# A 128x128 triangular inverse by doubling: 32x32 blocks in four row tiles for the first levels, and the even steps written out

## What is computed

```
def step(state, inp):
    rt, wt, kt, vt, kkt, at = inp
    sa = einsum('bhvk,bhk->bhv', state, -kkt)
    state = state * wt[:, :, None, :] + sa[..., None] * (kkt * at)[:, :, None, :] + vt[..., None] * kt[:, :, None, :]
    return state, einsum('bhvk,bhk->bhv', state, rt)
```

## Time and profile before

| | |
|---|---|
| median of three runs | 2680.56 us (2678.67 to 2683.04) |
| the profiled execution | 2677.95 us, span 2676.2 us |
| TensorE busy in the span | 2593.6 us, 97% |
| VectorE, ScalarE, GpSimd busy | 1908.0 (71%), 1268.7 (47%), 373.4 (14%) |
| chain that ended last | TensorE 88%, VectorE 7%, issue 2%, ScalarE 2% |
| even steps in the timeline | from 59.94 us (step 0) to 590.37 us |

### The profile page before, as it was taken

One profiled execution on the slowest core, in us unless ns is written; L12 is line 12 of the kernel. 1 busy time (PEld: TensorE's weight loads), 2 busy tenths in 40 slices (PEclk: granted clock), 3 DMA queues, 4 the chain that ended last, 5 costly groups with the idle time before them and its releaser, 6 DMA issues.

```text
span 2676.2 us, 48399 instructions
## 1 busy us (share of the span) xinstructions
PE 2593.6 (97%) x17454; PEld 2297.0 (86%) x17454; DVE 1908.0 (71%) x2983; ACT 1268.7 (47%) x1721; POOL 373.4 (14%) x376
## 2 busy tenths in 40 slices
PE   8998989989999999999999999998999999999998
PEld 8887888878888888888888888887888888888886
DVE  6666666666766666656789999997676666666666
ACT  6444444445554344334465555554555434433444
POOL 0111111112110011001112121111111001100112
PEclk9999999999999999999999999998999999999999
DMA  6222222234555555555454444443455555555543
GB/s 263 97 99 95 97 97 97 87 121 165 197 188 189 188 188 188 188 188 188 164 197 173 157 157 157 157 157 142 169 192 188 191 186 188 188 188 188 188 168 131
DMA packets 65866, 437.98 MB, mean 164 GB/s; under 512 B 9440, under 2 KB 10848, under 8 KB 17120
## 3 DMA queue, kind: packets, MB, share of 16 engines
q1 hardware_dynamic: 61920, 435.84, 46.1%
q10 hardware_dynamic: 3840, 0.70, 0.1%
HBM read 434.41 MB, written 2.10 MB: 163 GB/s over the span
## 4 chain that ended last, share of the span: by engine, by line
PE 88%; DVE 7%; issue 2%; ACT 2%; DMA 0%; DVEq 0%; ACTq 0%; SPq 0%; POOL 0%; POOLq 0%
PE acc L318 49%; PE acc L353 27%; PE acc L315 5%; PE mixer_banks L1593 2%; DVE w_low L308 1%; PE mixer_banks L1305 1%; PE mixer_banks L1397 1%; PE mixer_banks L1410 1%; ACT w_high L303 1%; ACT arena L651 0%; PE mixer_banks L1412 0%; PE acc L330 0%; DVE arena L1005 0%; DVE arena L993 0%; DVE arena L932 0%
## 5 line engine op out<-in xcount | busy, mean ns | idle before, releaser
L308 DVE TENSOR_TENSOR w_low<-w_raw,w_high 128x1024 fp32r<-128x1024 f32 x838 | 1053.1, 1258 | 413.3 <-ACT w_high L303 401.4
L303 ACT ACTIVATE w_high<-w_raw 128x1024 fp32r<-128x1024 f32 x837 | 881.6, 1058 | 938.8 <-PE acc L353 923.3
L318 PE MATMUL acc<-h_split,w_high 128*128 128x512 f32 x3840 | 977.0, 394 | 6.3 <-DVE arena L375 6.3
L318 PEld LDWEIGHTS acc<-h_split,w_high 128*128 128x128 f32 x3840 | 688.6, 189 | 128.4 <-issue 5.4
L353 PEld LDWEIGHTS acc<-h_split,w_low 128*128 128x128 f32 x4576 | 629.9, 191 | 39.7
L353 PE MATMUL acc<-h_split,w_low 128*128 128x256 f32 x4576 | 660.0, 282 | 0.0
L318 PE MATMUL acc<-mix_split,w_high 128*128 128x512 f32 x1908 | 493.0, 396 | 1.9 <-DVE mix_split L1267 1.4
L318 PEld LDWEIGHTS acc<-mix_split,w_high 128*128 128x128 f32 x1908 | 343.0, 190 | 64.7 <-issue 2.5
L480 POOL TENSOR_TENSOR arena<-arena,norm_scale 128x256 f32<-128x256 f32 x152 | 150.9, 993 | 1457.2 <-DVE arena L375 1456.0
L353 PEld LDWEIGHTS acc<-mix_split,w_low 128*128 128x128 f32 x1876 | 260.8, 191 | 21.3
L353 PE MATMUL acc<-mix_split,w_low 128*128 128x256 f32 x1876 | 267.1, 282 | 0.0
(11 more groups left out here) (257 smaller groups left out, 1684.1 us busy)
## 6 DMA issues: line engine op xcount, KB each, us to landing
w_raw<-w_gu SPq DMA_DIRECT2D x176, 1024.0 KB, 4.8
w_raw<-w_down SPq DMA_DIRECT2D x64, 1024.0 KB, 4.9
w_raw<-w_odd SPq DMA_DIRECT2D x64, 1024.0 KB, 4.8
w_raw<-w_even SPq DMA_DIRECT2D x49, 1024.0 KB, 4.8
w_raw<-w_down SPq DMA_DIRECT2D x32, 768.0 KB, 4.3
w_raw<-w_odd_out SPq DMA_DIRECT2D x16, 1024.0 KB, 4.8
w_raw<-w_even_out SPq DMA_DIRECT2D x10, 1024.0 KB, 4.8
w_raw<-w_even_out SPq DMA_DIRECT2D x6, 896.0 KB, 4.6
```

Of the source, the lines that this page charges most:

```text
L303: act.activation(wh[:, self.res, ks], raw[:, self.raw, ks], ACT.Copy).then_inc(high_done, 1)
L308: dve.tensor_tensor(wl[:, self.res, ks], raw[:, self.raw, ks], wh[:, self.res, ks].bitcast(F32), ALU.subtract).then_inc(low_done, 1)
L318: pe.matmul(acc[self.acc][:, 0:2 * T], wh[:, self.res, k], flat(both), start=k == 0, stop=stop)
```

## The change

- The inverse holds four diagonal 32x32 quarter blocks. Levels 1 to 4 are matmuls on four diagonal 32x32 tiles; `z` has 16 matmuls a level for 8, `txt` 32 for 16. `Xb`, `Zs`, `Ld` and the two halves of `TT` have half the columns. `Ld` is made by four copies for two. `m3` computes four quarter blocks for two half blocks.
- Level 5 becomes an off-diagonal block step like level 6: 8 matmuls in `z`, 12 in `txt`, three `tensor_scalar` pieces on VectorE. GpSimd spreads `TT` into `T11` (new, 64 rows) and `Tf` after level 4, two instructions for one; GpSimd's masking for level 5 is gone.
- `z` writes to bank 1 instead of bank 2, and the wait for `KTR` moves from `z(1)` to behind `z(6)`.
- ScalarE: the square of the keys (L612) comes before the table load and `high(3)`.
- VectorE: `evacuate(-1)` comes before `low(2)` instead of before `low(3)`.
- TensorE: `dense(16)` and `dense(16)` instead of `dense(8)` and `dense(24)`; in step 7 the second half of a block waits for `rw_end`.
- ScalarE and VectorE have all eight steps written out; GpSimd keeps its loop.

```
-        TT = take(4, 2, 64)
-        Xb = take(2, 4, 64)
-        Zs = take(4, 64)
-        Ld = take(4, 64)
+        TT = take(4, 2, 32)
+        Xb = take(2, 4, 32)
+        Zs = take(4, 32)
+        Zh = take(4, 64)
+        T11 = take(4, 64)
+        Ld = take(4, 32)
...
+        QUARTERS = [slice(q, q + 32) for q in range(0, P, 32)]
...
-                pool.wait_ge(S["rw_L"], 2 * j + 2)
-                for l in range(1, LEVELS - 1):
+                pool.wait_ge(S["rw_L"], 4 * j + 4)
+                for l in range(1, LEVELS - 2):
...
-                pool.wait_ge(S["rw_TT"], 7 * j + 6)
-                pool.tensor_tensor(Tf.rearrange("p n (a b) -> p n a b", a=2), TT[:, :, 1].unsqueeze(2).broadcast_to([P, 4, 2, 64]),
...
+                pool.wait_ge(S["rw_TT"], 9 * j + 5)
+                for out, rows, which, parts in ((T11, HALVES[0], 0, 2), (Tf, slice(0, P), 1, 4)):
+                    pool.tensor_tensor(out[rows].rearrange("p n (a b) -> p n a b", a=parts),
...
-                act.preload_act_table_set("natural_log_exp_and_others")
-
-                high(3)
                 act.wait_ge(S["rw_xv"], j + 1)
                 act.activation(d3[:, 2], xm[:, 1], ACT.Square, scale=pj[:, P_KK:P_KK + 1]).then_inc(S["rw_sq"], 1)
+                act.preload_act_table_set("natural_log_exp_and_others")
+                high(3)
...
-                for r in HALVES:
+                for r in QUARTERS:
                     act.activation(Ld[r], LTR[r, :, r], ACT.Copy).then_inc(S["rw_L"], 1)
...
+                    if l < LEVELS - 1:
+                        act.activation(flat(Zs), bank(1)[:, 0:P], ACT.Copy).then_inc(S["rw_Zs"], 1)
+                    else:
+                        act.activation(flat(Zh)[HALVES[1]], bank(1)[HALVES[1], 0:256], ACT.Copy).then_inc(S["rw_Zs"], 1)
...
-            even_step(0, even_block(0))
-            with act.Fori(0, 3) as i:
-                for e in range(2):
-                    even_step(1 + 2 * i + e, even_block(1 + e, i))
-            even_step(7, even_block(7), more=False)
+            for j in range(NRW):
+                even_step(j, even_block(j), more=j < NRW - 1)
...
+                evacuate(-1)
                 low(2)
...
-                evacuate(-1)
                 low(3)
...
+                    dve.wait_ge(S["rw_Tf"], 2 * j + 2)
+                    if l == LEVELS - 2:
+                        for out, rows, at in ((T11[:, :, 0:32], 1, 0), (Tf[:, :, 32:64], 0, P), (Tf[:, :, 96:P], 2, P)):
+                            rows = QUARTERS[rows]
+                            dve.tensor_scalar(out[rows], bank(0)[rows, at:at + P].rearrange("p (n c) -> p n c", n=4), -1.0, None, ALU.mult).then_inc(S["rw_TT"], 1)
...
+                            if ks[0] >= HALF:
+                                pe.wait_ge(S["rw_end"], NRW)
...
-                dense(8)
+                dense(16)
...
-                dense(24)
+                dense(16)
...
-                for b in range(2):
+                for b in range(4):
...
-                            last = pe.matmul(bank(4 + h)[HALVES[b], 64 * c:64 * c + 64], AR[rows, c, 0, HALVES[b]], bk[rows, 0, at], start=True, stop=True)
+                            last = pe.matmul(bank(4 + h)[QUARTERS[b], 32 * c:32 * c + 32], AR[rows, c, 0, QUARTERS[b]], bk[rows, 0, at], start=True, stop=True)
...
+                    if l == LEVELS - 2:
+                        for n in range(4):
+                            for q in (0, 2):
+                                r = QUARTERS[q]
+                                last = pe.matmul(bank(1)[QUARTERS[q + 1], 32 * n:32 * n + 32], LTR[r, n, QUARTERS[q + 1]], TT[r, n, 0], start=True, stop=True)
...
-                        for r in HALVES:
-                            last = pe.matmul(bank(2)[r, 64 * n:64 * n + 64], Xb[r, l % 2, n], TT[r, n, 0], start=True, stop=True)
+                        for r in QUARTERS:
+                            last = pe.matmul(bank(1)[r, 32 * n:32 * n + 32], Xb[r, l % 2, n], TT[r, n, 0], start=True, stop=True)
...
+                    if l == LEVELS - 2:
+                        low, high = QUARTERS[1], QUARTERS[3]
+                        for n in range(4):
+                            at = slice(P + 32 * n, P + 32 * n + 32)
+                            pe.matmul(bank(0)[low, 32 * n:32 * n + 32], TT[low, n, 1], Zs[low, n], start=True, stop=True)
+                            pe.matmul(bank(0)[QUARTERS[2], at], Zs[high, n], TT[high, n, 1], start=True, stop=True)
+                            last = pe.matmul(bank(0)[QUARTERS[0], at], Zs[low, n], TT[low, n, 1], start=True, stop=True)
...
-                        o = bank(0)[:, n * P:(n + 1) * P]
-                        for r in HALVES:
-                            pe.matmul(o[r, 0:64], TT[r, n, 1], Zs[r, n], start=True, stop=True)
-                        for r in HALVES:
-                            last = pe.matmul(o[r, 64:P], Zs[r, n], TT[r, n, 1], start=True, stop=True)
+                        o = bank(0)[:, n * 64:(n + 1) * 64]
+                        for r in QUARTERS:
+                            pe.matmul(o[r, 0:32], TT[r, n, 1], Zs[r, n], start=True, stop=True)
+                        for r in QUARTERS:
+                            last = pe.matmul(o[r, 32:64], Zs[r, n], TT[r, n, 1], start=True, stop=True)
...
+                waits(pe, 2 * j + 2, "rw_KTR")
                 pe.wait_ge(S["rw_kbn"], j + 1)
```

More of the change, by code:

```diff
@@ L39 @@
 C_HALF = C_CAUSAL + 3 * P
-C_LOW0 = C_HALF + 6 * 64
-C_IDH = C_LOW0 + 64
-C_END = C_IDH + 64
+C_LOW0 = C_HALF + 5 * 32
+C_IDQ = C_LOW0 + 32
+C_QUART = C_IDQ + 32
+C_END = C_QUART + P
 P_MU, P_W0, P_A0, P_KK, P_KA, P_RK = 0, 3, 4, 5, 6, 7
@@ L69, in shape_constants @@
         c[:, C_LVL + l * P:C_LVL + (l + 1) * P] = m
-        halves = lambda a: np.concatenate([a[:64, :64], a[64:, 64:]])
-        if l < 6:
-            c[:, C_HALF + 64 * l:C_HALF + 64 * (l + 1)] = halves(m)
+        quarters = lambda a: np.concatenate([a[q:q + 32, q:q + 32] for q in range(0, P, 32)])
+        if l < 5:
+            c[:, C_HALF + 32 * l:C_HALF + 32 * (l + 1)] = quarters(m)
         if l == 0:
-            c[:, C_LOW0:C_LOW0 + 64] = halves(m.T)
-            c[:, C_IDH:C_IDH + 64] = halves(np.eye(P))
+            c[:, C_LOW0:C_LOW0 + 32] = quarters(m.T)
+            c[:, C_IDQ:C_IDQ + 32] = quarters(np.eye(P))
+    c[:, C_QUART:C_QUART + P] = s // 32 == t // 32
     c[:, C_TRI:C_TRI + P] = s < t
@@ L995, in even_step @@
                 for h in range(2):
-                    dve.tensor_tensor(TT[:, 2 * h:2 * h + 2, 0], bank(4 + h)[:, 0:P].rearrange("p (c k) -> p c k", c=2),
-                                      bc(cst[:, C_LOW0:C_LOW0 + 64], 2), ALU.mult).then_inc(S["rw_T0"], 1)
-                dve.wait_ge(S["rw_L"], 2 * j + 2)
+                    dve.tensor_tensor(TT[:, 2 * h:2 * h + 2, 0], bank(4 + h)[:, 0:64].rearrange("p (c k) -> p c k", c=2),
+                                      bc(cst[:, C_LOW0:C_LOW0 + 32], 2), ALU.mult).then_inc(S["rw_T0"], 1)
+                dve.wait_ge(S["rw_L"], 4 * j + 4)
                 dve.tensor_tensor(TT[:, :, 1], Ld, bc(half_mask(0), 4), ALU.mult).then_inc(S["rw_T0"], 1)
@@ L1097, in _ @@
                 Block(EVEN + u + 2).low(dve, 1)
-            even_step(0, even_block(0))
-            with dve.Fori(0, 3) as i:
-                for e in range(2):
-                    even_step(1 + 2 * i + e, even_block(1 + e, i))
-            even_step(7, even_block(7), more=False)
+            for j in range(NRW):
+                even_step(j, even_block(j), more=j < NRW - 1)
             added = [KT]
@@ L1384, in z @@
                 def z(l):
-                    pe.wait_ge(S["rw_TT"], 7 * j + l)
+                    pe.wait_ge(S["rw_TT"], 9 * j + l)
                     if l == LEVELS - 1:
                         for n in range(4):
-                            last = pe.matmul(bank(2)[64:P, 64 * n:64 * n + 64], LTR[0:64, n, 64:P], TT[0:64, n, 0], start=True, stop=True)
+                            last = pe.matmul(bank(1)[64:P, 64 * n:64 * n + 64], LTR[0:64, n, 64:P], T11[0:64, n], start=True, stop=True)
                         last.then_inc(S["rw_Z"], 1)
                         return
-                    pe.wait_ge(S["rw_X"], 5 * j + l)
-                    if l == 1:
-                        pe.wait_ge(S["rw_KTR"], 2 * j + 2)
+                    if l == LEVELS - 2:
[3 more added lines that the diff above has]
+                                last = pe.matmul(bank(1)[QUARTERS[q + 1], 32 * n:32 * n + 32], LTR[r, n, QUARTERS[q + 1]], TT[r, n, 0], start=True, stop=True)
+                        last.then_inc(S["rw_Z"], 1)
+                        return
+                    pe.wait_ge(S["rw_X"], 4 * j + l)
                     for n in range(4):
-                        for r in HALVES:
-                            last = pe.matmul(bank(2)[r, 64 * n:64 * n + 64], Xb[r, l % 2, n], TT[r, n, 0], start=True, stop=True)
+                        for r in QUARTERS:
```

(8 more changed lines are left out.)

25 lines of the change are left out of this document (12 added, 13 removed).

## The result

The changed kernel takes 2659.28 us (median of four runs, 2655.67 to 2660.41) beside 2681.47 us for the kernel before in the same session: ratio 0.9917, 95% interval 0.9902 to 0.9932, 22.2 us less. The forecast was 2656.0, a gain of 24.6. In what follows "gain" is (1 - ratio) x 2680 us against the kernel before of the same session; where steps are compared, the times are of the profiled executions. Each interval is about 4.4 us of gain to either side, so differences of a few us between two runs are read from the steps and not from the medians.

What follows compares the result with a forecast made beforehand. The prediction took VectorE to bound each even step's first half and TensorE the second. Eight steps at 2.2 us (17.6) plus 7.0 for written-out steps made 24.6 off 2680.56: 2656.0 us, own range 2650 to 2662.

Steps and rivals of the forecast that it cites:

- part 1: Square before the table load, `dense(16)`, `evacuate(-1)` earlier: TensorE's 2 us wait for the square is given back later, 0 us.
- part 2: VectorE's half of each even step with smaller tiles: net -0.2 us a step, bounds -0.4 and +0.3.
- part 3: Smaller tiles in TensorE's half, levels 3 to 5: 2.0 us less a step.
- part 4: Steps written out: gaps at VectorE's L928, where the loop of two steps goes back twice, vanish; 7.0 us less.
- split in halves: In step 2 VectorE limits 188 to 221 us, TensorE 221 to 254; TensorE savings count fully only in the second.
- this point doesn't move by more than its own shortening: TensorE's need of `rw_T0` at L1380, where it waits for VectorE: VectorE's work before it stays the same in total.
- rival C: ScalarE's new order or the GpSimd cover runs out, a full microsecond late in each step: 2664 us, chance 0.06.
- rival E: TensorE's clock falls after waits that come together, 1 us in each step: 2664 us, chance 0.05.
- A: TensorE's records on four tiles limited to 0.0167 us each, saving only 0.3 us a step in its half: 2670 us, chance 0.12.
- B: More tiles bring no gain, 0.029 us a record being TensorE's own limit: slower, 2693 us, chance 0.06.
- D: The 7 us at the loop's turns stay, because written-out code is fetched late there too: 2663 us, chance 0.04.
- F: VectorE's first half shortens by more than thought, 1 us a step: 2648 us, chance 0.05.

Runs made afterwards that it cites:

- old_order: Changed kernel with part 1 undone: square behind `high(3)`, `evacuate(-1)` behind `low(2)`, `dense(8)` and `dense(24)` again; 2654.05 us, ratio 0.9897 to the kernel before.
- written_out_only: Kernel before with one edit: ScalarE and VectorE have their eight even steps written out; 2666.86 us, ratio 0.9949.
- txt1_twice: Changed kernel with the 32 matmuls of `txt(1)` sent twice in every step, in VectorE's half; 2655.65 us, ratio 0.9912 to the kernel before.
- txt3_twice: Changed kernel with the 32 matmuls of `txt(3)` sent twice in every step, in TensorE's half; 2668.23 us, ratio 0.9956 to the kernel before.
- moved_old_tiles: Kernel before, 64x64 tiles kept, with steps written out and the orders and dense counts of `move9`; 2646.50 us, ratio 0.9876.
- move9: `ktr_dense12` with nine more dense tiles a step moved ahead of the attention weights' transposes; 2620.41 us, ratio 0.9774 to the kernel before.
- loops: Changed kernel with ScalarE and VectorE looping again over steps 1 to 6, three rounds of two; 2670.20 us, ratio 0.9964 to the kernel before.
- ktr_first: Changed kernel with VectorE's two `KTR` products moved ahead of its wait for ScalarE's `Ld` copies; 2649.87 us, ratio 0.9887 to the kernel before.
- dense8: Changed kernel with only TensorE's counts put back to `dense(8)` and `dense(24)`; 2650.57 us, ratio 0.9896 to the kernel before.
- ktr_dense12: `ktr_first` with `dense(12)` and `dense(20)` around the norm of the keys (8 and 24 in step 0); 2642.27 us, ratio 0.9858 to the kernel before.
- shifted_code: Changed kernel with the 32 matmuls of `txt(1)` sent twice in step 0 only, so later TensorE code stands 64 records further on; 2653.82 us, one run.

## Why the prediction came out right in sum and wrong in its terms

| term | forecast us | measured us | by |
|---|---|---|---|
| part 1, order and `dense(16)` | 0 | +4.7 | first halves, after less `old_order` |
| part 2, first half by small tiles | -1.6 | -2.4 | first halves, `old_order` less `written_out_only` |
| part 3, TensorE's half | -16.0 | -10.1 | second halves, after less before |
| part 4, written-out steps | -7.0 | -13.6 | first halves, `written_out_only` less before |
| behind the even stage | 0 | +4.0 | profiled executions |
| sum | -24.6 | -17.4 | spans: -17.6; medians: -22.2 |

That the sum came near is in part luck: parts 2 and 4 brought 7.4 us more than forecast, and parts 1 and 3 and the time behind the stage took away 14.6.

**What bounds the kernel: right.** The split in halves held. `txt1_twice` shows that TensorE's work in the first is free, `txt3_twice` that it counts in full in the second.

**Part 1: the step that failed is "this point doesn't move by more than its own shortening".** I followed `AR` and `bk` to `m1` and held VectorE's order there for fixed. Its place in the order is fixed, its inputs are not: L948 (L954 in after) takes the product of L1346 right behind `low(2)`, and I moved that product eight tiles later without asking who waits for it. I looked for the wait on TensorE, and it came up on VectorE. The thin slack of ScalarE's square did hold (rival C has no row: L971, the piece that takes `rn`, doesn't wait), and the gain on the square was zero as said.

**Part 2: right in kind.** The four `Ld` copies take 1.31 us (forecast 1.3); VectorE's L1007 0.52 for 1.01. The net is -0.3 a step for -0.2.

**Part 3: the prices were right, the arrival wasn't.** `z` 0.38 (forecast 0.41), `txt` 0.68 (0.66). Undisturbed second halves are 30.37 us (step 4), 2.08 less than before, where I had said 2.0. But only four of the eight come within 0.2 us of that. What is missing, 6.5 us, is a term that the sum did not have: 2.6 us of waits for nothing in `txt(4)` and near it, and the rest stands beside stretches at half clock, as behind 418.00 in step 5 and from 536 to 541 us in step 7. `written_out_only` and `moved_old_tiles` have a mean clock of 1.00 from 60 us to the end of the stage and none of these waits. Rows of the stage in before, after, `written_out_only` and `moved_old_tiles`, in this order:

```profile
60.00:590.00 530.00, 485.93 (x5121) 432.99 (x5120) 351.87 (x680) 227.18 (x465) 67.75 (x62) 0.98 0.27 95
```

```profile
60.00:568.00 508.00, 458.57 (x6720) 407.35 (x6718) 336.09 (x694) 222.63 (x481) 46.33 (x62) 0.98 0.29 99
```

```profile
60.00:577.00 517.00, 479.44 (x5123) 427.20 (x5122) 349.19 (x681) 226.86 (x465) 69.52 (x62) 1.00 0.28 97
```

```profile
60.00:556.00 496.00, 480.23 (x5123) 427.40 (x5122) 348.65 (x680) 223.57 (x465) 64.99 (x62) 1.00 0.29 101
```

Before has the same mean as after, and yet its second halves are untouched: its half-clock stretches fell where VectorE carried the chain. So rival E was right in kind, and its clause "most of such a loss lies in VectorE's half and is hidden" holds for before and not for after. All ten kernels with the small tiles have half-clock stretches inside the stage, from one in `move9` to eleven in `loops`; the two kernels with the old tiles and written-out steps have none before its end. That the tiles make the difference is likely, but not shown, and a wait alone doesn't decide it: the same wait of 3.0 us at the stage's end was followed by 1.00 in before and 0.50 in after.

**Part 4: the step that failed is "these are the two places where the loop goes back".** The turns cost what I read: the first halves of steps 3 and 5 are 3.8 and 3.0 us longer than those of steps 2 and 4. But steps 2 to 6 all cost 1.2 us more than in written-out form and step 7 0.8, and it could be read ahead: step 2 takes 65.93 us, and the same timeline gives 64.74 for step 1. I took step 2 as the ordinary step; step 1 would have been the one to compare with.

**The rivals.** A and B fell with `txt3_twice`: 0.008 us a record on four tiles. By the Trainium skill (TensorE: Matmul & The Clock Gate, "Wait — 56ns, not 53.3ns?") matmuls don't start closer than about 25 ns. Here 64 records, which are 32 matmuls, are sent in 0.52 us, 0.016 a matmul. So the rule can hold for one tile of the array (0.033 us a record) and not for the engine, and the measurement decides. D fell: no wait of 3 us is left at the turns. F fell: the first halves by the tiles are 0.3 us a step shorter, not 1; `ktr_first` shows that an earlier `KTR` could have given another 0.9.

**The marks named ahead.** Steps of 63.7: the mean is 63.6, but from 62.7 to 65.6, not all alike. Waits of 1.3 before `m1` (0.69), 1.4 before the scores (1.20), 2 before `z(2)` (2.15). No "issue" at L928: right, and the gaps came elsewhere.

**Behind the even stage.** The 4.0 us that after loses there are not the tiles. Its rows are the same, with half-clock stretches at 568.2 and 646.7 us that before does not have, and the time behind the stage follows that in the other kernels: 2085.0 to 2085.7 us in `dense8`, `ktr_dense12`, `loops` and `shifted_code`, all with small tiles, whose first sixteen records there take 2.17 or 2.18 us; 2088.6 and 2089.1 in `written_out_only` and `moved_old_tiles`, with the old tiles, where the sixteen take 2.65 and 3.79.

**What stays open.** What decides where the clock falls, and whether TensorE's waits for nothing are the loading of its code.

## What to carry to other kernels

Work saved on the engine that is full in one half of a step is worth its time only there; in the other half it turns into idle time until work is moved into it, and moving nine tiles gave 22 us, as much as the whole change. Before a product is put behind other work, look up who takes it: the wait that vanishes on one engine comes up on the consumer. When a loop is to be written out, compare a step inside it with one outside it, not only the turn with the other steps.

## What the runs showed of the hardware that I had not expected

- Four 32x32 tiles of TensorE's array run side by side, writing one bank: 64 float32 records in 0.52 us, 0.008 each. One tile takes a record each 0.033 us, against 0.058 for 64 columns and 0.115 for 128.
- In straight-line code TensorE waited 0.2 to 1.5 us for nothing in or shortly behind such dense stretches, up to seven times in eight steps; 64 records more in step 0 made those of steps 5 and 6 vanish, and with TensorE's program unchanged (`ktr_first`) they stayed at the same instructions. With the 64x64 tiles there was none.
- Inside a loop, VectorE's last four pieces of a step and the first of the next took 1.2 us more than in written-out code, beside "issue" gaps of 3.90 and 3.49 us at the loop's turns; in `loops` the first halves inside the loop lost 0.5 to 0.7.
- After a wait of 3.0 us at the same place, the granted clock was 1.00 in one kernel and 0.50 in the other, and sixteen records took 2.17 and 3.78 us.
